# Expert rows fetched as u halves by token and v halves by selection; 32-column v matmuls

## The reference

```python
def block(hb):                                   # 128 tokens at a time
    q = (hb @ w_pq).reshape(TOK_BLOCK, PEER_HEADS, 2, PEER_DHALF)
    s = jnp.einsum('thpd,hpnd->thpn', q, sub_keys).astype(jnp.float32)
    ...                                          # two top-16 lists and the top 16 of their 256 sums
    idx = jnp.take_along_axis(cand_i, pos, axis=-1)
    gate = jax.nn.softmax(top_s, axis=-1).astype(hb.dtype)
    u = expert_u[idx]
    act = jax.nn.gelu(jnp.einsum('thkd,td->thk', u, hb), approximate=False)
    vv = expert_v[idx]
    return jnp.einsum('thk,thkd->td', gate * act, vv)
```

## Time and profile before

| What | Value |
|---|---|
| median of three runs | 3163.95 us (3162.23 to 3174.32) |
| span of the profiled execution | 3168.1 us |
| its time beyond the span | not given |
| PE busy | 2617.8 us |
| DVE busy | 1722.4 us |
| POOL busy | 582.0 us |
| bytes moved by the gathers | 536.90 MB |

### The profile page before, as it was taken

One profiled execution on the slowest core, in us unless ns is written; L12 is line 12 of the kernel. 1 busy time (PEld: TensorE's weight loads), 2 busy tenths in 40 slices (PEclk: granted clock), 3 DMA queues, 4 the chain that ended last, 5 costly groups with the idle time before them and its releaser, 6 DMA issues. The chain is left out here.

```text
span 3168.1 us, 23012 instructions
## 1 busy us (share of the span) xinstructions
PE 2617.8 (83%) x7588; PEld 1312.0 (41%) x7588; DVE 1722.4 (54%) x3834; ACT 320.4 (10%) x765; POOL 582.0 (18%) x516
## 2 busy tenths in 40 slices
PE   6799399889997777867777777787789978999998
PEld 4455399844452233322323323333334433444443
DVE  3644865432077677576676677555535647333304
ACT  1123121010010000100001000100010010111100
POOL 0000000000003434434434444344410000000000
PEclk9899599689998888889889898899889988999999
DMA  3201000032189999989999999999942121122210
GB/s 117 93 7 54 0 1 1 1 139 80 64 296 384 379 379 395 380 364 385 390 387 367 380 373 387 379 393 410 417 179 80 60 105 68 53 80 80 80 67 27
DMA packets 126790, 655.73 MB, mean 207 GB/s; under 512 B 9456, under 2 KB 12144, under 8 KB 60912
## 3 DMA queue, kind: packets, MB, share of 16 engines
q0 software_dynamic: 73728, 536.90, 41.9%
q1 hardware_dynamic: 52976, 117.74, 10.3%
HBM read 652.51 MB, written 2.10 MB: 207 GB/s over the span
## 5 line engine op out<-in xcount | busy, mean ns | idle before, releaser
L705 PE MATMUL PD<-AR,C 128*128 128x512 f32 x2048 | 1027.9, 661 | 349.2 <-DVE C L1511 348.9
L1654 POOL DMA_INDIRECT AR<-in_uv,C x512 | 581.8, 1136 | 1740.7 <-DVE C L1452 926.5
L1503 DVE CUSTOM_DVE_ANT_0 AR<-AR,HN 128x1024 f32<-128x1024 f32 x512 | 620.2, 1225 | 426.3 <-DMA AR<-in_uv,C 420.3
L705 PEld LDWEIGHTS PD<-AR,C 128*128 128x128 f32 x2048 | 423.7, 212 | 953.4 <-issue 494.7
L435 PE MATMUL PA<-HT,WR 128*128 128x512 f32 x736 | 327.2, 604 | 3.0 <-ACT HT L810 2.1
L435 PE MATMUL PA<-AR,WR 128*128 128x512 f32 (+1 forms) x720 | 314.1, 605 | 6.4 <-ACT AR L881 4.9
L435 PEld LDWEIGHTS PA<-HT,WR 128*128 128x128 f32 x736 | 141.9, 194 | 179.1 <-issue 175.3
L435 PEld LDWEIGHTS PA<-AR,WR 128*128 128x128 f32 (+1 forms) x720 | 138.5, 194 | 181.6 <-issue 178.7
L979 ACT ACTIVATE SC<-SC 128x2 f32<-128x2 f32 x256 | 51.9, 204 | 1276.4 <-DVE SC L1503 1276.4
L1511 DVE TENSOR_SCALAR C<-C,SC 128x128 f32<-128x128 f32 x512 | 148.6, 349 | 1.6 <-ACT SC L979 1.6
L1621 DVE TENSOR_SCALAR HT<-HN,V 128x512 f32<-128x512 f32 x44 | 24.0, 546 | 198.2 <-ACT HN L1008 198.2
(11 more groups left out here) (322 smaller groups left out, 2274.4 us busy)
## 6 DMA issues: line engine op xcount, KB each, us to landing
WR<-in_w_ada SPq DMA_DIRECT2D x12, 2048.0 KB, 7.8
WR<-in_w_in SPq DMA_DIRECT2D x11, 2048.0 KB, 7.7
WR<-in_w_up SPq DMA_DIRECT2D x11, 2048.0 KB, 7.9
WR<-in_w_down SPq DMA_DIRECT2D x5, 2048.0 KB, 7.8
WR<-in_w_pq SPq DMA_DIRECT2D x4, 2048.0 KB, 8.0
AR<-in_uv,C POOLq DMA_INDIRECT x512, 9.4
WR<-in_w_o SPq DMA_DIRECT2D x2, 2048.0 KB, 7.9
WR<-in_w_out SPq DMA_DIRECT2D x2, 2048.0 KB, 7.7
```

Source lines behind the costliest of these rows:

```text
L705: ins = nc.tensor.matmul(acc[half], DG[:, j, :], UV[:, j, D + 512 * half:D + 512 * half + 512], start=False, stop=False)
L1503: ttr(UV[:, j, 0:D], UV[:, j, 0:D], HN[:, t, :], 1.0, 0.0, ALU.mult, ALU.add, DOT[:, g, j % GRP:j % GRP + 1]).then_inc(s["dots"], 1)
L1654: nc.gpsimd.indirect_dma_start(UV[:, turn % RING, :], None, uv, bass.IndirectOffsetOnAxis(ap=IDX[:, t % 2, i:i + 1], axis=0),).then_inc(uv ...
```

## The change

Viewed as rows of 1024 numbers, `uv` has u of expert e at row 2e and v at row 2e+1. The two are now gathered apart, half a megabyte each, into a ring `ROWS` of 16 slots in the same memory.

- **u by token**, as before: gather k fetches for each token of the tile the u of its selection k. The dots of a whole tile are collected in `DOTS` (128 columns), one Gelu and one product with the gates follow, and PE transposes the result, so that it lies with a selection to each partition and a token to each column (`WT`). The indices are transposed too (`turn_index`, `index_rows`).
- **v by selection**: a gather fetches for one token the v of all its 128 selections, one to each partition. The weights are a matrix of 128 x 32 that is zero but for the one column of the token (`quad` makes four of them, for tokens q, 32+q, 64+q and 96+q, with one instruction). PE multiplies with 32 columns of weights, so that the four products of a quad write four groups of 32 partitions of the same bank. v slots are given back four at a time, by a quad.
- **Order**: u of tile 0 comes alone, with all of `select` for tile 1 between its dots. Then v of tile t alternates with u of tile t+1, gather by gather, with `select` for tile t+2. v of tile 3 comes alone. `layer_rows` stands at the end of each tile's v. POOL issues 1024 gathers in place of 512.

```diff
-RING = 8
-GRP = 2
+RING = 16
+QUADS = P // 4
+WSLOTS = 8
+def u_row(t, k):
+    return k if t == 0 else NSEL * (2 * t - 1) + 2 * k
+def v_row(t, r):
+    return NSEL * (2 * t + 1) + (2 * r + 1 if t < NT - 1 else r)
+def row_user(i):
+    turn, r = divmod(i - NSEL, 2 * NSEL)
+    if i < NSEL:
+        return "u_used", i + 1
+    if turn == NT - 1:
+        return "v_used", QUADS * turn + r // 4 + 1
+    if r % 2 == 0:
+        return "u_used", NSEL * (turn + 1) + r // 2 + 1
+    return "v_used", QUADS * turn + r // 8 + 1
...
-TURNS = NSEL // RING
-NORM_AT, TURN_AT = 2, 4
-SELECT_AT = (3, 5, 7, 8, 10, 11, 13, 14)
...
-        UV = AR[:, 0:RING * 2048].rearrange("p (r n) -> p r n", r=RING)
+        ROWS = AR[:, 0:RING * D].rearrange("p (r n) -> p r n", r=RING)
+        DOTS = ar(22528, NSEL)
+        WT = ar(22656, P)
...
-        DG = lvl[:, 0:1024].rearrange("p (r n) -> p r n", r=RING)
+        WQ = lvl[:, 0:1024].rearrange("p (r j n) -> p r j n", r=WSLOTS, j=4)
...
-            fours = cc("ones")[0:1, :].unsqueeze(1).broadcast_to([1, 4, P])
-            for t in range(NT):
+            def turn_index(t):
+                pe.wait_ge(s["idx"], t + 1)
+                transposes("d", [SS[t][:, 0:NSEL]])
+            turn_index(0)
+            turn_index(1)
+            for t in range(NT):
+                pe.wait_ge(s["wtok"], t + 1)
+                transposes("d", [DOTS])
+                if t > 0:
+                    turn_block("xn3", t - 1, "aa")
                 acc = [bank("d"), bank("d")]
-                for half in range(2):
...
-                                               stop=True))
+                for q in range(QUADS):
+                    pe.wait_ge(s["wquad"], QUADS * t + q + 1)
+                    for half in range(2):
+                        for j in range(4):
+                            i = v_row(t, 4 * q + j)
+                            if half == 0:
+                                pe.wait_ge(row_full[i % RING], 16 * (i // RING + 1))
+                            ins = nc.tensor.matmul(acc[half][32 * j:32 * j + 32, :], WQ[:, q % WSLOTS, j, :],
+                                                   ROWS[:, i % RING, 512 * half:512 * half + 512],
+                                                   start=(q == 0), stop=(q == QUADS - 1))
+                        if q == QUADS - 1:
+                            full("d", ins)
+                    if q < QUADS - 1:
+                        ins.then_inc(s["v_used"], 1)
+                pe.drain().then_inc(s["v_used"], 1)
+                if t + 2 < NT:
+                    turn_index(t + 2)
...
-            for t in range(NT):
...
-            roots(ffv(NT - 1))
+            gate_exp(0)
+            for t in range(NT):
+                act.wait_ge(s["u_used"], NSEL * (t + 1))
+                tell(A(DOTS, DOTS, ACT.Gelu), "gelud")
+                if t + 1 < NT:
+                    gate_exp(t + 1)
+                if t > 0:
+                    turned_both(t - 1)
+                roots(ffv(t))
...
-                    if t >= 2:
-                        dve.wait_ge(s["uv_used"], NSEL * (t - 1))
...
-                    link(nc.vector.tensor_copy(IDX[:, t % 2, :], acc_[0]), "idx")
+                    link(ts(IDX[:, t % 2, :], acc_[0], 2.0, None, ALU.mult), "idx")
...
-            for t in range(NT):
...
-                                       ALU.mult, ALU.mult).then_inc(s["diag"], 1)
+            def index_rows(t):
+                b = take()
+                link(ts(IDXT[:, t % 2, :], b[:, 0:P], 2.0, 1.0, ALU.mult, ALU.add), "d_free")
+                tell(dve.nop(), "idxt")
+            def dot(t, k):
+                i = u_row(t, k)
+                row = ROWS[:, i % RING, :]
+                dve.wait_ge(row_full[i % RING], 16 * (i // RING + 1))
+                tell(ttr(row, row, HN[:, t, :], 1.0, 0.0, ALU.mult, ALU.add, DOTS[:, k:k + 1]), "u_used")
+            def weights(t):
+                dve.wait_ge(s["gelud"], t + 1)
+                tell(tt(DOTS, DOTS, GATE[:, t % 2, :], ALU.mult), "wtok")
+                b = take()
+                link(nc.vector.tensor_copy(WT, b[:, 0:P]), "d_free")
+            def quad(t, q):
+                if QUADS * t + q >= WSLOTS:
+                    dve.wait_ge(s["v_used"], QUADS * t + q - WSLOTS + 1)
+                tell(stt(WQ[:, q % WSLOTS, :, :], cc("iota").unsqueeze(1).broadcast_to([P, 4, 32]), float(q),
+                         WT.rearrange("p (j q) -> p j q", j=4)[:, :, q:q + 1].broadcast_to([P, 4, 32]),
+                         ALU.is_equal, ALU.mult), "wquad")
+            index_rows(0)
+            gates(0)
+            for k in range(NSEL):
+                if k % 16 == 0:
+                    select(1, k // 16)
+                dot(0, k)
+            index_rows(1)
+            for t in range(NT):
+                weights(t)
+                if t + 1 < NT:
+                    gates(t + 1)
+                for q in range(QUADS):
+                    quad(t, q)
+                    if t + 1 < NT:
+                        for k in range(4 * q, 4 * q + 4):
+                            dot(t + 1, k)
+                    if t + 2 < NT and q % 4 == 2:
+                        select(t + 2, q // 4)
                 for half in range(2):
                     b = take()
                     xs = X[:, t, 512 * half:512 * half + 512]
                     link(tt(xs, xs, b, ALU.add), "d_free")
-            layer_rows("xn3", NT - 1, X[:, NT - 1, :], HN[:, NT - 1, :])
+                layer_rows("xn3", t, X[:, t, :], HN[:, t, :])
+                if t + 2 < NT:
+                    index_rows(t + 2)
...
-            for t in range(NT):
...
-                    ).then_inc(uv_full[turn % RING], 16)
+            rows = uv.rearrange("e (h d) -> (e h) d", h=2)
+            def gather(i, index):
+                if i == RING // 2:
+                    pool.wait_ge(s["peer_clear"], 1)
+                if i >= RING:
+                    name, count = row_user(i - RING)
+                    pool.wait_ge(s[name], count)
+                nc.gpsimd.indirect_dma_start(
+                    ROWS[:, i % RING, :], None, rows, bass.IndirectOffsetOnAxis(ap=index, axis=0),
+                ).then_inc(row_full[i % RING], 16)
+            def token(r):
+                return 32 * (r % 4) + r // 4
+            for t in range(NT + 1):
+                if t < NT:
+                    pool.wait_ge(s["idx"], t + 1)
+                if t > 0:
+                    pool.wait_ge(s["idxt"], t)
+                for k in range(NSEL):
+                    if t < NT:
+                        gather(u_row(t, k), IDX[:, t % 2, k:k + 1])
+                    if t > 0:
+                        gather(v_row(t - 1, k), IDXT[:, (t - 1) % 2, token(k):token(k) + 1])
```

More of the change, by code:

```diff
@@ L153, in constants @@
     put("invfreq", (np.float32(10000.0) ** (-np.arange(HALF, dtype=np.float32) / np.float32(HALF)))[None, :])
-    put("iota", np.arange(TOPK)[None, :])
+    put("iota", np.arange(32)[None, :])
     cnt = [1.0 / np.minimum(np.arange(16) + 1, w) for w in POOL]
@@ L204, in build @@
                  "ct", "x1t", "tmid", "ycomb",
-                 "topk", "idx", "dots", "geluv", "diag", "uv_used", "csil",
+                 "topk", "idx", "idxt", "u_used", "geluv", "gelud", "wtok", "wquad", "v_used", "csil",
                  "bufs", "conv", "convsq", "silu_in", "silu", "pooled", "merged",
@@ L212, in build @@
         w_sem = [ctx.enter_context(nc.semaphore(f"w_slot{i}")) for i in range(NWR)]
-        uv_full = [ctx.enter_context(nc.semaphore(f"uv_full{i}")) for i in range(RING)]
+        row_full = [ctx.enter_context(nc.semaphore(f"row_full{i}")) for i in range(RING)]
         n = {nm: 0 for nm in names}
@@ L279, in small @@
             sc_at[0] += w
-            assert sc_at[0] <= 1240, sc_at[0]
+            assert sc_at[0] <= 1224, sc_at[0]
             v = SC[:, a:a + w]
@@ L1486, in _ @@
             tell(dve.nop(), "peer_clear")
-            for t in range(NT):
[L1489 to L1498, removed]
-                            if g < RING // GRP:
-                                for j in range(GRP * g, GRP * g + GRP):
-                                    dve.wait_ge(uv_full[j], it * 16 + 16 * (NSEL // RING * t + 1))
-                                    ttr(UV[:, j, 0:D], UV[:, j, 0:D], HN[:, t, :], 1.0, 0.0, ALU.mult, ALU.add,
-                                        DOT[:, g, j % GRP:j % GRP + 1]).then_inc(s["dots"], 1)
-                            if g >= 1:
-                                dve.wait_ge(s["gelu"], it * (RING // GRP) + (NSEL // GRP * t + g))
-                                for j in range(GRP * (g - 1), GRP * g):
-                                    sel_ = GATE[:, t % 2, bass.ds(it * RING + j, 1)]
-                                    ts(DG[:, j, :], ident, GEL[:, g - 1, j % GRP:j % GRP + 1], sel_,
-                                       ALU.mult, ALU.mult).then_inc(s["diag"], 1)
```

21 lines of the change are left out of this document (5 added, 16 removed), and 2 rows, old and new, of the table JOBS.

## The result

The changed kernel took 3303.3 us (median of 4 runs, 3296.6 to 3307.6), the kernel before 3163.1 beside it: ratio 1.0445, 95% interval 1.0417 to 1.0472. It is 140 us slower; 3317 was forecast.

A forecast was written before the change was run, and what follows sets the result against it. The prediction took the expert stage's DMA transfers as the bound, with DVE, POOL, then PE limiting successive stretches after the change. The last add moves from 2345.3 to 2498, so 3164 + 153 = 3317 us; range 3222 to 3400.

The forecast's parts named there:

- last dot of stretch 0: u of tile 0 alone: DVE is the limit, 147 us dots plus 56 us selection, 203 us, until 1153.
- one half row, mixed stretches: u and v alternating: POOL is the limit at 1.136 + 0.30 = 1.44 us per half row, taken as 1.45.
- last u dot: End of the mixed stretches: 1165 + 1088 + 4 = 2257 for the last issue, its dot ending at 2262.
- from there to the last add: v of tile 3 alone: hand-over 13.5 us, then 32 quads of 6.9 us, 222 us.
- last add: End of the expert stage: starts at 2498 against 2345.3 before, +153 us, all of it moving the kernel's end.
- The ring is then full, 16 half rows ahead: End of stretch 0: POOL has run 16 half rows ahead of the dots, streaming again at 1165 after the hand-over.
- issues in step with dots: Mixed stretches: every second issue held to 1.91 us, a half row costing 1.73, 210 us more, 3527; chance 0.07.
- the 1.37 that I took for the transfers: Half-row price where the DMA engines are the limit: 1.36 to 1.42 us, taken as 1.37.
- PE cold: PE at the lower clock, 1.2 GHz: a quad takes 13.9 us, more than its rows' 11.6; 3537 us; chance 0.07.
- By the nearest row I take 0.87: Last stretch: a product of 32 weight columns costs 0.87 us, one after the other; 32 quads 222 us.
- the rival with 0.34: Products of a quad overlap side by side: last stretch set by transfers, 179 us, add at 2441, 3260 us; chance 0.34.

The follow-up runs named there:

- undisturbed session: Another session, in which the unaltered changed kernel was measured again beside the kernel before: 3213.9 us, ratio 1.0174.
- e1: Kernel before with each whole-row gather split into two half rows, order and arithmetic unchanged: 3258.9 us, ratio 1.0291.
- e4: Changed kernel with DVE waiting for the end of its own dot after each dot of tile 0: 3201.6 us, ratio 1.0117.
- e3: Changed kernel with each dot over 128 of the 1024 columns, the rest left out: 3095.1 us, ratio 0.9783.
- e2: Changed kernel with all four products of a quad written to the same 32 partitions, one after the other: 3297.8 us, ratio 1.0438.
- disturbed session: The session of the result, in which the changed kernel took 3303.3 us, ratio 1.0445 to the kernel before.
- e5: Changed kernel with DVE waiting for its own dot's end after every dot of all four tiles: 3288.6 us, ratio 1.0394.
- repetition: The changed kernel itself run once more, nothing altered, in another session: 3213.9 us, ratio 1.0174.
- e6: Changed kernel with added waits in the first stretch on the dot four before, so without a gap between dots: 3307.5 us, ratio 1.0452.
- e7: Changed kernel with each v slot given back after its own row's two products instead of after the quad's eight: 3305.9 us, ratio 1.0447.
- e8: Changed kernel with gaps after every dot and v slots given back row by row, e5 and e7 together: 3288.0 us, ratio 1.0381.
- repeated e4: Changed kernel with DVE's wait after each dot of tile 0, run again beside the changed kernel in one session: 3205.8 us, ratio 1.0145.
- e10: Kernel before with each dot over 128 of the 1024 columns, the rest left out: 3070.2 us, ratio 0.9702.
- e11: Kernel before, complete, with each tile's token row copied to PSUM, so dots read one operand there: 3157.5 us, ratio 0.9982.

## Why the prediction was right, and where it was not

The last add is the end less 821 to 823 us, so each step can be read on its way to it. Times in us from the span's start, forecast, in the session of the result, and of the same kernel in the undisturbed session:

| step | forecast | result | undisturbed |
|---|---|---|---|
| last dot of stretch 0 | 1152 | 1160.6 | 1167.9 |
| one half row, mixed stretches | 1.45 | 1.47 | 1.37 |
| last u dot | 2261 | 2291.3 | 2223.4 |
| from there to the last add | 237 | 187 | 167 |
| last add | 2498 | 2478.0 | 2390.8 |

**The direction and its cause: right.** Half rows double POOL's issues, POOL's busy time went to 1131.6 us (about 1150 forecast) and its waits for PE fell from 774.5 us to 6.1 (6.4 undisturbed, without the 67 us of "remote"). e1 shows the price without the new order: +95 us.

**Stretch 0: the limit was right, one step failed.** DVE sets it, and 203 us were forecast; from the first dot to the start of the last it took 201, the first starting 10 us later than I put it, because the first step of the selection of tile 1 stands ahead of it. "The ring is then full, 16 half rows ahead" failed: at the last dot POOL had issued 130, not 144 (142 in e4, whose gaps let an issue in at every dot). An unheld issue and its gap take 1.24 us, against 203 / 128 = 1.59 us per dot, so I saw no limit in POOL; but where the dots are dense it makes one issue per 2.29 us. The sum lets gather 146 leave at 1165; it left at 1183.9, 19 us later, after POOL had made up what the full ring would have held. This was my rival "issues in step with dots", right in mechanism and in the 1.99 us, but in stretch 0, not in the mixed stretches where I had placed it.

**Mixed stretches: right for a reason that I did not know.** 1.47 against 1.45 looks like a hit. Undisturbed it is 1.37, of which POOL accounts for 1.062 + 0.30; the packets alone could have gone at 1.28, as in e3. So the 1.37 that I took for the transfers, from a DMA share of 0.95 as if that were full, was too high as well, though it set nothing here. I had put the issue at its old mean of 1.136, arguing that dots fill the same share of the time. They do (45% of the stretch before and undisturbed after), and no fewer issues start inside one (39% before, 47% after); but these start later in the dot, 0.86 us after its start in the mean against 0.61, and so are held shorter: 1.18 us in all against 1.40. Why they fall later the traces do not explain. The term was 0.08 x 750 = 60 us too large. In the session of the result 75 us came back (1130.7 against 1055.5 from the last dot of stretch 0 to the last u dot): 58 of them are more idle time of POOL, most of it the pauses, and 17 are longer issues (1.084 us). Of the rival "PE cold" the first half came: the granted clock fell to 0.66 to 0.73 in these stretches, from 0.87 and 0.88. No cost of it is seen: PE was busy for 197 to 222 us of 367 to 385, and undisturbed, at 0.68 to 0.72, POOL waited for it for 6.4 us in the whole span.

**Last stretch: wrong.** "By the nearest row I take 0.87" failed, and the rival with 0.34 was the right one. From the last u dot to the last add 237 us were forecast and 187 and 167 measured. Twelve passes of a quad take 2.39 us (timeline of PE, the undisturbed run), where twelve in a row would take 12 x 0.433 = 5.2:

```profile
2291.48 2.39 PE L733 MATMUL PD<-AR,C 128*32 128x512 f32 x12 [0.24 <-DMA AR<-in_uv,C]
```

The Trainium skill ("TensorEngine Tiling (Array Packing)", section "Tiling Modes") says that tiles operate independently and in parallel; here the trace agrees (twelve passes in 2.39 us). In e2, which takes the four groups away, the passes follow each other at 0.429 us and the stretch takes 235 us: the 237 of the forecast was right for products one after the other, and what failed is that they would not overlap. The 1 x 512 row was the wrong neighbour: it had nothing beside it to overlap with. With overlap I had 179 us; 167 were measured undisturbed, at 402 GB/s.

**The sum.** That 3303.3 lies near 3317 is in good part luck: the last u dot came 30 us late and 50 were made up after it, and 89 us of the result come and go with the session. Undisturbed, the kernel takes 3213.9, 8 us under my range. The account that the runs support is: half rows +95 (e1), the new order back some -45 (the changed kernel undisturbed, +51, against e1), the disturbed session +89. What the new order gives back goes with POOL's waits for PE, 94.6 us in e1 and 6.4 undisturbed. At half rows the new order is thus faster than the old one; no run compares the two orders at whole rows.

**What stays open** is the cause of the pauses. One of them, in the last stretch of the changed kernel (timelines of PE, PEld and POOL):

```profile
2365.42 0.62 PE L733 MATMUL PD<-AR,C 128*32 128x512 f32 x1 [0.23 <-DMA AR<-in_uv,C]
...
2366.64 0.60 PE L733 MATMUL PD<-AR,C 128*32 128x512 f32 x1 [0.60 <-issue]
...
2367.33 0.11 PEld L733 LDWEIGHTS PD<-AR,C 128*32 128x32 f32 x1 [0.59 <-issue]
...
2368.03 0.84 PE L733 MATMUL PD<-AR,C 128*32 128x512 f32 x1 [0.78 <-issue]
...
2368.73 0.12 PEld L733 LDWEIGHTS PD<-AR,C 128*32 128x32 f32 x1 [1.29 <-issue]
...
2369.43 4.25 PE L733 MATMUL PD<-AR,C 128*32 128x512 f32 x25 [0.56 <-issue]
...
2369.75 0.94 POOL L1703 DMA_INDIRECT AR<-in_uv,C  x1 [4.13 <-remote]
```

From 2366.64 to 2369.43 PE starts one weight load or pass every 0.70 us, where nothing that the profile shows holds them, and POOL stands still for 4.1 us before its next issue. In the last stretch of the changed kernel and of e5 this recurs at every 20th gather (912 to 1012). Three signs go together in every trace of these orders: the pauses, POOL and DVE waiting for "remote", and missing records (10,657 landings in the trace of the changed kernel where its repetition has 17,516). The last two may be one sign, since the profile infers who ended a wait from such records. The changed kernel, e5, e6, e7 and e8 have them; e1 to e4, the repetition and the repeated e4 do not. The kernel before stood at 3163 to 3165 in all sessions, and its trace from the session of the result has as many landings as that of e10 (9,328); whether the short loop that it has on PE is what protects it was not tried. The one execution of e10 at 3290.3 us left no trace, so it is open whether it is the same thing.

## What to carry to other kernels

Halving the size of a gather doubles the work of the engine that issues it; before doing so, add up busy time plus the gap after each issue, and set it against the transfer. A DMA share near 1 does not prove that the transfers are the limit: shorten the suspected consumer once, and see whether the same bytes move faster. Compare variants only within one session, with the unchanged kernel and the parent variant in it: here a difference of 100 us between two sessions looked like a property of the kernel and was none, and the unchanged kernel, at the same time in both, did not give it away.

## What the runs showed of the hardware

- A gather's issue that starts inside a dot with both operands in SBUF is held to its end (up to 1.99 us instead of 0.94). With one operand in PSUM it is not, while the dot takes the same 1.22 us: the 182 issues of e11 that start inside a dot take 0.94 us in the mean, the 199 of the kernel before 1.38. A dot that starts inside an issue is not held (1.22 us in the mean over 381 in the changed kernel). Two issues of e11 beside dots; the second starts 0.39 us into one:

```profile
1142.00 0.94 POOL L1660 DMA_INDIRECT AR<-in_uv,C  x1 [0.78 <-PE PD L706]
1142.18 1.22 DVE L1509 CUSTOM_DVE_ANT_0 AR<-AR,PA 128x1024 f32<-128x1024 f32 x1 [1.64 <-DMA AR<-in_uv,C]
...
1148.48 1.22 DVE L1509 CUSTOM_DVE_ANT_0 AR<-AR,PA 128x1024 f32<-128x1024 f32 x1 [1.25 <-DMA AR<-in_uv,C]
1148.87 0.94 POOL L1660 DMA_INDIRECT AR<-in_uv,C  x1 [0.78 <-PE PD L706]
```

- Gathered 4 KB rows move nearly as fast as 8 KB rows when they are issued in time: 402 to 406 GB/s in e3 behind its first stretch, 413 to 417 in e10.
- A DMA share of 0.95 stood beside 356 GB/s in the changed kernel and 0.94 beside 380 in the kernel before, a share of 1.02 beside 405 in e3. The gathered 4 KB packets took 175 ns in the mean in the changed kernel, 172 undisturbed and 164 in e3, so part of the share is packets that take longer and move no more; why they do is not shown.
- Four products of 32 columns of weights, written to four groups of 32 partitions, overlap on TensorE: twelve passes in 2.39 us, against one pass per 0.429 us in e2, where all write the same group.
